# Rope parts of three heads stacked on 96 partitions, swapped weight columns in place of rotations, and taps in another order

## What is computed

```python
proj = h @ w_in
conv_in, c_q, c_kv, k_r, d_q, d_k, d_v = jnp.split(proj, cuts, axis=-1)
y_conv = conv_module(conv_in, ...)     # GLU, 31 causal taps, layer norm, SiLU, product
q = (rms_norm(c_q, q_norm) @ w_uq).reshape(B, S, 6, 64 + 32)
q = concat([q[..., :64], apply_rope(q[..., 64:], pos)])
kv = (rms_norm(c_kv, kv_norm) @ w_ukv).reshape(B, S, 6, 64 + 64)
k = concat([kv[..., :64], apply_rope(k_r, pos) for every head])
y_mla = softmax(q @ k.T / sqrt(96), causal) @ kv[..., 64:]
y_diff = (softmax(q1 @ k1.T - alibi) - lam * softmax(q2 @ k2.T - alibi)) @ d_v
x = x + concat([y_conv, y_mla, y_diff]) @ w_out
# apply_rope: (x1, x2) -> (x1 cos - x2 sin, x1 sin + x2 cos) on the halves of 32
```

## Time and profile before

| | us |
|---|---|
| median of 3 runs | 1302.74 (1300.78 to 1306.17) |
| the profiled execution | 1304.77 |
| its span | 1302.9 |
| PE busy in the span | 1243.3 |
| DVE / ACT / POOL busy | 1020.0 / 822.2 / 144.8 |

### The profile page before, as it was taken

The page is one execution under the profiler, slowest core; times in us unless marked ns, Lnnn a source line. Parts: engine busy times, 40 slices in busy tenths (PEclk is TensorE's granted clock), DMA queues, the critical chain, the costliest instruction groups (busy, mean ns, idle before and its releaser), DMA issues.

```text
span 1302.9 us, 18352 instructions
## 1 busy us (share of the span) xinstructions
PE 1243.3 (95%) x6658; PEld 1052.8 (81%) x6658; DVE 1020.0 (78%) x1107; ACT 822.2 (63%) x862; POOL 144.8 (11%) x139
## 2 busy tenths in 40 slices
PE   6898899999899887999999999999999999999997
PEld 6875799999897676888888888888888888888885
DVE  5886555544568756889989889889889889889886
ACT  5357444444543754777777777677677777777774
POOL 2860000000049102000000000000000000000000
PEclk9888999999899797999999999999999999999999
DMA  9400665555351119999999999999999999999961
GB/s 331 155 15 1 200 201 187 186 176 189 117 178 65 49 46 376 367 369 371 364 366 358 365 359 362 360 369 359 352 374 358 350 377 349 358 372 359 357 238 48
DMA packets 176165, 349.64 MB, mean 268 GB/s; under 512 B 5719, under 2 KB 63637, under 8 KB 176116
## 3 DMA queue, kind: packets, MB, share of 16 engines
q1 hardware_dynamic: 173852, 341.27, 73.9%
q0 software_dynamic: 2064, 7.17, 1.5%
q10 hardware_dynamic: 200, 0.54, 0.1%
HBM read 346.87 MB, written 2.10 MB: 268 GB/s over the span
## 4 chain that ended last, share of the span: by engine, by line
PE 87%; DVE 7%; ACT 3%; issue 2%; DMA 0%; SPq 0%; POOL 0%; POOLq 0%; DVEq 0%; ACTq 0%
PE bank L1482 26%; PE bank L1484 26%; PE bank L1483 26%; PE bank L1797 1%; DVE cv L1127 1%; PE bank L1579 1%; DVE lo_ring L1006 1%; DVE xn L1127 1%; PE bank L1619 1%; ACT hi_ring L690 1%; PE bank L1789 1%; PE bank L1763 1%; PE bank L1778 1%; PE bank L1561 1%; PE bank L1790 1%
## 5 line engine op out<-in xcount | busy, mean ns | idle before, releaser
L1011 DVE TENSOR_TENSOR lo_ring<-raw_m,hi_ring 128x2048 fp32r<-128x2048 f32 x168 | 382.9, 2287 | 53.0 <-ACT hi_ring L696 52.9
L696 ACT ACTIVATE hi_ring<-raw_m 128x2048 fp32r<-128x2048 f32 x168 | 323.0, 1923 | 84.0 <-PE bank L1484 84.0
L1482 PE MATMUL bank<-hi_ring,hT_hi 128*128 128x512 f32 (+2 forms) x896 | 337.2, 376 | 0.0
L1484 PE MATMUL bank<-hi_ring,hT_lo 128*128 128x512 f32 (+2 forms) x896 | 329.5, 368 | 0.0
L1483 PE MATMUL bank<-lo_ring,hT_hi 128*128 128x512 f32 (+2 forms) x896 | 329.1, 367 | 0.0
L1011 DVE TENSOR_TENSOR lo_ring<-raw_a,hi_ring 128x2048 fp32r<-128x2048 f32 x96 | 219.1, 2290 | 32.7 <-ACT hi_ring L696 32.7
L696 ACT ACTIVATE hi_ring<-raw_a 128x2048 fp32r<-128x2048 f32 x96 | 183.4, 1918 | 54.6 <-PE bank L1484 54.6
L1006 DVE TENSOR_TENSOR lo_ring<-raw_a,hi_ring 128x2048 fp32r<-128x2048 f32 (+2 forms) x59 | 132.2, 2244 | 94.8 <-ACT hi_ring L690 94.8
L1482 PEld LDWEIGHTS bank<-hi_ring,hT_hi 128*128 128x128 f32 x896 | 169.6, 189 | 30.3 <-DVE lo_ring L1011 2.4
L1484 PEld LDWEIGHTS bank<-hi_ring,hT_lo 128*128 128x128 f32 x896 | 169.5, 189 | 28.9
L1483 PEld LDWEIGHTS bank<-lo_ring,hT_hi 128*128 128x128 f32 x896 | 169.8, 189 | 27.2 <-issue 0.5
(11 more groups left out here) (277 smaller groups left out, 1409.0 us busy)
## 6 DMA issues: line engine op xcount, KB each, us to landing
raw_m<-in_w_down_exp SPq DMA_DIRECT2D x80, 1024.0 KB, 5.9
raw_a<-in_w_up_exp SPq DMA_DIRECT2D x48, 1024.0 KB, 6.3
raw_m<-in_w_gate_exp SPq DMA_DIRECT2D x48, 1024.0 KB, 6.2
raw_a<-in_w_gate_exp SPq DMA_DIRECT2D x40, 1024.0 KB, 6.2
raw_m<-in_w_up_exp SPq DMA_DIRECT2D x40, 1024.0 KB, 7.2
raw_a<-in_w_in SPq DMA_DIRECT2D x12, 1024.0 KB, 8.0
raw_a<-in_w_gate_dense SPq DMA_DIRECT2D x11, 1024.0 KB, 5.4
raw_a<-in_w_up_dense SPq DMA_DIRECT2D x11, 1024.0 KB, 5.8
```

The lines of the kernel that those rows point to most:

```text
L696: A(hi_of(NA + j), t, ACT.Copy).then_inc(hi_ready, 1)
L1011: V.tensor_tensor(lo_of(NA + j), expert_slot(i, j)[0], hi_of(NA + j).bitcast(F32), ALU.subtract).then_inc(lo_ready, 1)
L1482: M(o, lh, rh, start=start, stop=False)
L1484: return M(o, ll, rh, start=False, stop=stop)
```

## The change

- Queries and keys are kept in parts: `q_nope`, `k_nope` (64 rows a head, two heads on 128 partitions) and `q_rope` (32 rows a head, three heads on 96 partitions). `kr` holds the rope key three times.
- `w_uq` and `w_ukv` come in as `wq_nope`, `wq_rope`, `wk_nope`, `w_v`. POOL copies `wq_rope` with its halves exchanged to `wq_swap`, and a product with it takes the place of the rotation of `q_m`. The sign stands in the sine table.
- `load_small` has 7 DMAs in place of 3, and for layer 0 it stands behind piece 3.
- Each MLA score has four products in place of two.
- The six `bias` tables of layer 0 are made on ACT behind piece 3, no longer on DVE; `setup_lambda` moves from step 4 to step 6 of DVE.
- `TAPS_AT` goes from 0, 0, 8, 9, 8, 7, 5, 2, 1 to 0, 0, 8, 3, 8, 9, 6, 4, 2.

```diff
 N_PARAMS = 6
-MID = 16
+N_SMALL = 7
+MID = 13
+MID_MEAN, MID_VAR, MID_PW = 11, 12, 13
...
-MID_BANK = [0, 1, 2, 3, 0, 1, 2, 3, 0, 1, 2, 3, 0, 7, 7, 7]
-MID_ACT = {0: 1, 1: 2, 2: 3, 3: 4, 5: 5, 6: 6, 10: 8, 11: 9, 12: 10}
-ACT_MID_STEPS = 10
-ROPE_AT = {6: (0, 1), 7: (2,)}
-KEYS_AT = {7: (0, 1, 2)}
-DVE_MID_STEPS = 15
-MID_DVE = {4: 5, 7: 8, 8: 11, 9: 14}
+ACT_MID_STEPS = 7
+DVE_MID_STEPS = 9
...
 OUT_BANK = (5, 6, 4, 3)
-TAPS_AT = [0, 0, 8, 9, 8, 7, 5, 2, 1]
+TAPS_AT = [0, 0, 8, 3, 8, 9, 6, 4, 2]
...
 two[:, K_MASK:K_MASK + 3 * P] = np.where(dist < 0, MASKED, 0.0)
-two[:, K_DIST:K_DIST + 3 * P] = np.maximum(dist, 0)
+two[:, K_DIST:K_DIST + 3 * P] = np.where(dist < 0, -MASKED, dist)
...
 ang = np.arange(T, dtype=np.float32)[None, :] * freq[:, None].astype(np.float32)
-two[:NOPE, K_COS:K_COS + T] = 1.0
-for r in range(2):
-    lo = NOPE + r * half
-    two[lo:lo + half, K_COS:K_COS + T] = np.cos(ang)
-    two[lo:lo + half, K_SIN:K_SIN + T] = np.sin(ang)
+for r in range(3):
+    lo = r * ROPE
+    for a in range(ROPE):
+        two[NOPE + a, K_REP + lo + a] = 1.0
+        two[NOPE + (a + half) % ROPE, K_SWAP + lo + a] = 1.0
+    two[lo:lo + ROPE, K_COS:K_COS + T] = np.tile(np.cos(ang), (2, 1))
+    two[lo:lo + half, K_SIN:K_SIN + T] = -np.sin(ang)
+    two[lo + half:lo + ROPE, K_SIN:K_SIN + T] = np.sin(ang)
...
 sp.dma_start(w_pw[:], a["w_pw"][l].rearrange("(k p) n -> p k n", p=P)).then_inc(small_in, 16)
-sp.dma_start(w_uq[:], a["w_uq"][l].rearrange("(k p) n -> p k n", p=P)).then_inc(small_in, 16)
-sp.dma_start(w_ukv[:], a["w_ukv"][l]).then_inc(small_in, 16)
+for c in range(2):
+    heads = a["w_uq"][l, c * P:(c + 1) * P, :].rearrange("p (h d) -> p h d", h=HEADS)
+    sp.dma_start(wq_nope[:, c], heads[:, :, 0:NOPE]).then_inc(small_in, 16)
+    sp.dma_start(wq_rope[:, c], heads[:, :, NOPE:QD]).then_inc(small_in, 16)
+heads = a["w_ukv"][l].rearrange("p (h d) -> p h d", h=HEADS)
+sp.dma_start(wk_nope[:], heads[:, :, 0:NOPE]).then_inc(small_in, 16)
+sp.dma_start(w_v[:], heads[:, :, NOPE:]).then_inc(small_in, 16)
...
      lambda t, p=p: in_piece_view(t, p))
-if l == 0 and p == 2:
+if l == 0 and p == 3:
     load_small(0)
...
+pool.wait_ge(small_in, 16 * N_SMALL * (l + 1))
+half = ROPE // 2
+for m in range(2):
+    nc.gpsimd.tensor_copy(wq_swap[:, :, :, m * half:(m + 1) * half],
+                          wq_rope[:, :, :, (1 - m) * half:(2 - m) * half]).then_inc(w_swapped, 1)
...
     split(n0 + 3 + p)
+if l == 0 and p == 3:
+    for h in range(HEADS):
+        slope = 2.0 ** (-8.0 * (h + 1) / HEADS)
+        A(bias[:, h, :], dist, ACT.Copy, scale=-slope * HD ** 0.5).then_inc(bias_set, 1)
 if l == 0 and p == 1:
...
 if p == 5:
-    for r3 in range(3):
-        mid(1 + r3)
-        mid_inc(A(q_m[:, 2 * r3:2 * r3 + 2, :],
-                  bank[1 + r3][0:QD, :].rearrange("p (h t) -> p h t", h=2), ACT.Copy))
+    mid(2)
+    mid_inc(A(q_nope[:, 0:2, :], bank[1][:].rearrange("p (h t) -> p h t", h=2), ACT.Copy))
+    mid(3)
+    mid_inc(A(q_nope[:, 2, :], bank[2][:, 0:T], ACT.Copy))
...
 for t in range(TT):
-    mid(5 + t)
+    mid(6 + t)
...
-    act.wait_ge(mid_dve, DVE_MID_STEPS * l + 6)
-    mid_inc(A(k_m[NOPE:QD, :, :], kr[NOPE:QD, :].unsqueeze(1).broadcast_to([ROPE, HEADS, T]),
-              ACT.Copy))
-if p in KEYS_AT:
-    for r3 in KEYS_AT[p]:
-        mid(10 + r3)
-        mid_inc(A(k_m[0:NOPE, 2 * r3:2 * r3 + 2, :],
-                  bank[MID_BANK[10 + r3]][0:NOPE, :].rearrange("p (h t) -> p h t", h=2), ACT.Copy))
+if p == 7:
+    mid(8)
+    mid_inc(A(k_nope[:, 0:2, :], bank[1][:].rearrange("p (h t) -> p h t", h=2), ACT.Copy))
+    mid(9)
+    mid_inc(A(k_nope[:, 2, :], bank[2][:, 0:T], ACT.Copy))
...
 V.tensor_reduce(lam_dot[:], lam_prod[:], AX.X, ALU.add).then_inc(setup_v, 1)
-for h in range(HEADS):
-    slope = 2.0 ** (-8.0 * (h + 1) / HEADS)
-    V.scalar_tensor_tensor(bias[:, h, :], dist, -slope * HD ** 0.5, mask, ALU.mult, ALU.add).then_inc(setup_v, 1)
...
-def rope_q(pairs):
-    for r3 in pairs:
-        pair = q_m[:, 2 * r3:2 * r3 + 2, :]
-        wide = [QD, 2, T]
-        dve.wait_ge(mid_mm, MID * l + 8 + r3)
-        dve.wait_ge(mid_dve, ms_[0])
-        mids(V.tensor_tensor(pair, pair, cos.unsqueeze(1).broadcast_to(wide), ALU.mult))
-        mids(V.tensor_tensor(rot[:], bank[MID_BANK[7 + r3]][0:QD, :].rearrange("p (h t) -> p h t", h=2),
-                             sin.unsqueeze(1).broadcast_to(wide), ALU.mult))
-        dve.wait_ge(mid_dve, ms_[0])
-        mids(V.tensor_tensor(pair, pair, rot[:], ALU.add))
+def rope_k():
+    dve.wait_ge(mid_mm, MID * l + 2)
+    mids(V.tensor_tensor(kr[:], bank[3][0:QD, 0:T], cos, ALU.mult))
+    mids(V.tensor_tensor(rot[:, 0, :], bank[3][0:QD, T:2 * T], sin, ALU.mult))
+    dve.wait_ge(mid_dve, ms_[0])
+    mids(V.tensor_tensor(kr[:], kr[:], rot[:, 0, :], ALU.add))
+def rope_q():
+    wide = [QD, 2, T]
+    dve.wait_ge(mid_mm, MID * l + 6)
+    mids(V.tensor_tensor(q_rope[:], bank[0][0:QD, :].rearrange("p (h t) -> p h t", h=2),
+                         cos.unsqueeze(1).broadcast_to(wide), ALU.mult))
+    mids(V.tensor_tensor(rot[:], bank[3][0:QD, :].rearrange("p (h t) -> p h t", h=2),
+                         sin.unsqueeze(1).broadcast_to(wide), ALU.mult))
+    dve.wait_ge(mid_dve, ms_[0])
+    mids(V.tensor_tensor(q_rope[:], q_rope[:], rot[:], ALU.add))
...
     setup()
-if l == 0 and p == 4:
+if l == 0 and p == 6:
     setup_lambda()
...
-    dve.wait_ge(mid_mm, MID * l + 5)
-    mids(V.tensor_tensor(kr[:], kr[:], cos, ALU.mult))
-    mids(V.tensor_tensor(rot[:, 0, :], bank[0][0:QD, 0:T], sin, ALU.mult))
-    dve.wait_ge(mid_dve, ms_[0])
-    mids(V.tensor_tensor(kr[:], kr[:], rot[:, 0, :], ALU.add))
+    rope_k()
+if p == 6:
+    rope_q()
 if p == 7:
     maxima(0)
-if p in ROPE_AT:
-    rope_q(ROPE_AT[p])
 if p == 8:
...
 else:
-    q, kk = q_m[:, h, :], k_m[:, h, :]
+    r0, g0 = (h % 2) * NOPE, (h % 3) * ROPE
+    q, kk = q_nope[r0:r0 + NOPE, h // 2, :], k_nope[r0:r0 + NOPE, h // 2, :]
+    qr, kkr = q_rope[g0:g0 + ROPE, h // 3, :], kr[g0:g0 + ROPE, :]
 b = bank[S_BANK[u % 3]]
-M(b[:, 0:P], q[:, 0:P], kk[:, 0:P], start=True, stop=True)
-M(b[:, P:3 * P], q[:, P:2 * P], kk[:, :], start=True, stop=True).then_inc(s_mm, 1)
+M(b[:, 0:P], q[:, 0:P], kk[:, 0:P], start=True, stop=k < HEADS)
+if k >= HEADS:
+    M(b[:, 0:P], qr[:, 0:P], kkr[:, 0:P], start=False, stop=True)
+r = M(b[:, P:3 * P], q[:, P:2 * P], kk[:, :], start=True, stop=k < HEADS)
+if k >= HEADS:
+    r = M(b[:, P:3 * P], qr[:, P:2 * P], kkr[:, :], start=False, stop=True)
+r.then_inc(s_mm, 1)
...
     M(bank[0][:, T:2 * T], ones[:], sq_kv[:], start=True, stop=True).then_inc(mid_mm, 1)
+    if l == 0:
+        pe.wait_ge(params_in, 16 * N_PARAMS)
+    M(bank[3][0:QD, 0:T], replicate, kr[:], start=True, stop=True)
+    M(bank[3][0:QD, T:2 * T], swap, kr[:], start=True, stop=True).then_inc(mid_mm, 1)
 if p == 5:
-    pe.wait_ge(small_in, 48 * (l + 1))
-    pe.wait_ge(mid_dve, DVE_MID_STEPS * l + 3)
-    for r3 in range(3):
-        for hh in range(2):
-            h = 2 * r3 + hh
-            for c in range(2):
-                r = M(bank[1 + r3][0:QD, hh * T:(hh + 1) * T], w_uq[:, c, h * QD:(h + 1) * QD],
-                      cq[:, c, :], start=c == 0, stop=c == 1)
-        r.then_inc(mid_mm, 1)
-    mid_start(4)
-    M(bank[0][0:QD, 0:T], rotate, kr[:], start=True, stop=True).then_inc(mid_mm, 1)
+    pe.wait_ge(small_in, 16 * N_SMALL * (l + 1))
+    after_dve(2)
+    for pair in range(HEADS // 2):
+        for c in range(2):
+            r = M(bank[1 + pair // 2][:, (pair % 2) * T:(pair % 2 + 1) * T],
+                  wq_nope[:, c, 2 * pair:2 * pair + 2, :].rearrange("p h d -> p (h d)"), cq[:, c, :],
+                  start=c == 0, stop=c == 1)
+        if pair > 0:
+            r.then_inc(mid_mm, 1)
 if p == 6:
+    after_act(1)
+    for g in range(2):
+        for c in range(2):
+            r = M(bank[0][0:QD, g * T:(g + 1) * T], wq_rope[:, c, 3 * g:3 * g + 3, :].rearrange("p h d -> p (h d)"),
+                  cq[:, c, :], start=c == 0, stop=c == 1)
+    r.then_inc(mid_mm, 1)
+    after_dve(6)
+    pe.wait_ge(w_swapped, 2 * (l + 1))
+    for g in range(2):
+        for c in range(2):
+            r = M(bank[3][0:QD, g * T:(g + 1) * T], wq_swap[:, c, 3 * g:3 * g + 3, :].rearrange("p h d -> p (h d)"),
+                  cq[:, c, :], start=c == 0, stop=c == 1)
+    r.then_inc(mid_mm, 1)
     for t in range(TT):
-        mid_start(5 + t)
-        wv = w_ukv[:].rearrange("p (h n) -> p h n", h=HEADS)[:, :, NOPE:]
-        M(bank[1 + t][:, 0:HEADS * MV], ckv[:, t * P:(t + 1) * P], wv, start=True, stop=True
-          ).then_inc(mid_mm, 1)
-if p in ROPE_AT:
-    for r3 in ROPE_AT[p]:
-        mid_start(7 + r3)
-        M(bank[MID_BANK[7 + r3]][0:QD, :], rotate,
-          q_m[:, 2 * r3:2 * r3 + 2, :].rearrange("p h t -> p (h t)"), start=True, stop=True
-          ).then_inc(mid_mm, 1)
-if p in KEYS_AT:
-    for r3 in KEYS_AT[p]:
-        mid_start(10 + r3)
-        for hh in range(2):
```

(15 more changed lines are left out.)

48 lines of the change are left out of this document (26 added, 22 removed).

## The result

| | before | changed |
|---|---|---|
| median, us | 1303.4 (4 runs, 1300.78 to 1306.17) | 1295.86 (4 runs, 1295.3 to 1296.88) |
| ratio | | 0.9945, 95% interval 0.9925 to 0.9966 |
| the profiled execution, its span | 1304.77, 1302.9 | 1295.9, 1294.1 |

The forecast was 1296.2, and the total is met. The terms that make it up are not: two of them lie outside the bounds that they were given, and a gain that was not in the sum at all helps to make up the total. The profile shows where.

The account below looks back on a forecast made before the run. PE idles in the mixers behind DVE, and POOL is late next. Layer 0 -4.25, dense start +0.8 and layer 1 -3.1 give -6.55, so 1296.2 us on the median's scale; 8 in 10 between 1290 and 1303.5.

Parts of the forecast that it names:

- The join: DVE's join in the mixers' first stage starts when POOL ends: 3.95 us earlier in layer 0, 2.8 in layer 1.
- POOL's own gain: POOL's taps run faster with fewer rope operations beside them: about 0.3 us for each, some 0.6 in all.
- Behind the join: From DVE's join to the MLA slots, waits for PE vanish: 0.8 us gained a layer, between 0 and 1.1.
- the backlog: PE's queued scores and values behind the join, about 0.5 us, gone because PE idles while DVE waits for POOL.
- The MLA products: Second mixer stage: doubled score products in six MLA units cost 0.5 us net a layer, between 0.1 and 1.0.
- the pair of slot 3: Two units on different groups of 32 rows, 1.59 us where 2.6 was due, read as products on different rows overlapping.
- the rival of the low clock in the slots: MLA slots stay at low clock, plus 9.5 us in each layer, 1315 us in total; chance 0.10.
- Small loads: Weight loads in runs of 128 and 256 bytes cost 2.5 us more, upper end 5.2; hidden in layer 0.
- the cover of 3.1: Layer 0: slack between piece 4 landing at about 26.4 and ACT's split at 29.49, hiding 2.5 us of load cost.
- dense start: Layer 1's small loads ahead of the dense pieces make the dense part start 0.8 us later, between 0 and 3.5.
- Free of charge: Six biases on ACT fit its pause before piece 4, and POOL's two copies its idle 22.82 us; no cost.
- POOL slowed by 4 us in each layer: Rival: POOL gains nothing and two further jumps of 2 us come in its taps; about 1303.5 us, chance 0.10.

Follow-up runs that it names:

- e8: The kernel before, run once more unchanged for a second profiled execution; 1303.45 us.
- e5: The kernel before with only the new order of DVE's taps and the lambda setup two pieces later; 1298.21 us, ratio 0.9958.
- e3: The changed kernel with layer 1's seven small loads issued behind the eighth dense piece, no longer ahead of the first; 1295.74 us.
- e7: The changed kernel with MLA score products on all 128 and 96 rows, made right by key tiles with zeros in other heads' rows; 1293.58 us, ratio 0.9926.
- e6: The changed kernel with unread products on constants where PE would idle, ahead of scores(1) and of the norm transposes behind both mixers; 1297.66 us.
- e9: The changed kernel with the old order of DVE's taps over the nine pieces; 1296.97 us over 12 widely scattered runs, ratio 0.9952.
- e11: The changed kernel with zero-padded key tiles and layer 1's small loads behind the eighth dense piece; 1290.72 us, ratio 0.9903.
- e1: The changed kernel without the second product (32 rope rows) of each MLA score, so scores lack their rope part; 1293.52 us.
- e12: The changed kernel with zero-padded key tiles, late layer 1 small loads, and 20 of the second block's taps on POOL, not 22; 1288.3 us, ratio 0.9887.

## Why the prediction came out

**The join** (predicted -3.95 and -2.8). The reading of POOL as late next was right: in both layers the join waits for it, 3.16 and 3.56 us. In layer 0 it came 5.1 us earlier, 4.0 against e8. The size of POOL's own gain was off: 0.6 forecast, 53.75 to 51.65 us measured in layer 0 (2.1) and 0.9 in layer 1. In e5, which has the new order and the old rope work, POOL's run is 54.0 and 54.4. So what the change takes away is worth 1.9 to 2.4 us of POOL's run, not 0.3 for each of two triples. Not all of it is shown to be the rope operations. By an estimate from the timelines, tap by tap, the taps beside them are 1.1 to 1.4 us slower in all before and in e5, and 0 to 0.4 in the changed kernel; the rest lies beside the splits and has no cause here.

**Behind the join** (-0.8 a layer, bounds 0 to 1.1). This step left its bounds: the changed kernel gained 3.2 us in layer 0 and 0.8 in layer 1; e3 and e7 gained 2.5 and more in both. What was missing is the clock. From the join to the first MLA score, layer 0 before, layer 0 now and layer 1 now:

```profile
91.70:107.53 15.83, 15.83 (x58) 10.86 (x58) 10.55 (x51) 11.51 (x47) 0.00 (x0) 0.50 0.00 0
```

```profile
86.59:99.20 12.61, 11.96 (x49) 8.18 (x48) 10.30 (x49) 8.88 (x35) 0.00 (x0) 0.61 0.00 0
422.24:437.27 15.03, 14.00 (x48) 9.62 (x48) 10.39 (x49) 10.31 (x41) 0.56 (x1) 0.50 0.10 35
```

PE is busy nearly all the time, so it is the bound, and length times granted clock is 7.9, 7.7 and 7.5 us (7.5 to 8.2 in every kernel without the fillers of e6). At the same clock of 0.50 the gain is 0.8 us (layer 1; 0.8 and 0.9 in e9 and e11), which is what the backlog was priced at. The rest is the granted clock, which the sum held at its value before. The clock falls earlier against the join, at 82.8 where the join is at 86.59 (91.0 and 91.70 before), and part of the low stretch passes while DVE and PE wait for POOL. How long it stays low is not repeatable: 13.7 us in layer 0 and 20.5 in layer 1 in the changed kernel, 17.1 and 13.7 in e3, which is the same kernel up to there but for when the small loads are issued. Even the kernel before was 1.6 us faster there in one layer in e8. So that the new order brings the clock back sooner is likely and not shown.

**The MLA products** (+0.5 a layer, 0.1 to 1.0). The other step that failed: +2.5 and +2.8, and e1 shows it. The error is in one sentence. I read the pair of slot 3, 1.59 us for 2.6, as products on different rows that overlap, and carried that over to products on 64 and 32 rows. It doesn't hold where the number of rows changes from product to product. It also has the heads wrong: the rows meet for three of the six, not for two. And I let PE's idle in the slots cover the rest; with 1.42 us a unit the six add 8.5, and PE's waits in the slots before sum to 6.6. In the other direction the rival of the low clock in the slots was wrong: they run at 1.00.

```profile
108.00:112.00 4.00, 4.00 (x18) 2.50 (x19) 2.73 (x11) 1.86 (x7) 0.00 (x0) 1.00 0.00 0
```

**Small loads.** The short runs cost 2.2 us (2.5 forecast). In layer 0 the cover of 3.1 should have left 0.6; instead ACT's fifth split waits a little:

```profile
29.79 1.91 ACT L695 ACTIVATE hi_ring<-raw_a 128x2048 fp32r<-128x2048 f32 x1 [0.45 <-DMA raw_a<-in_w_in]
```

That is 0.3 later than before; four more issues on SP were not in the sum. At the dense start the wait cost 0.9 us (6.84 for 5.94; 0.8 forecast). The stretch up to layer 1 is longer by 1.0 more; I put that to the half clock, which was not in the sum, since e5 has the same 3.4 us of it, no such wait, and 1.1 more than before. The nearness of 2.5 and 2.2 is in part luck. The window that 8.7 ns a run came from shows only 93 packets under 512 bytes by the DMA view (14 to 17 us, before), where the changed kernel has 3026 (21 to 24 us): the short runs of `wr` and the lambdas show no packets of their size there, only 189 larger ones on the software queue.

**Free of charge.** The biases on ACT took 2.58 us ahead of an idle of 0.56, so they cost nothing, as said. So did the copies on POOL.

**Signs.** Of the signs that were named, these came: no idle before the query products, full clock to 79 us, a join released by POOL behind a wait of over 3 us, MLA slots at full clock. These did not: the join of layer 0 is at 86.59 and not between 87 and 89, ACT's fifth split has a DMA wait, and its wait for the second dense piece stayed at 1.09 us; the one for the first grew, from 0.63 to 2.65. And POOL's run of 51.65 in layer 0 lies below the 52 to 55 that was set as the mark of being wrong (layer 1: 52.5): the size of POOL's gain is what failed there, not its place as the bound.

**Slips in the working.** The query products before were at half clock only to 60.3 us, for 5.0 of their 7.88. And for POOL slowed by 4 us in each layer the terms give 1296.2 + 8 = 1304.2, not 1303.5. Neither moves the forecast.

**Not in the sum at all.** 2.1 us in the experts' stage (e8), and 1.2 where the clock came back sooner behind the router in this execution.

Added up with the profiled span, forecast and measured: layer 0 -4.25 and -5.8, dense start +0.8 and +1.9, layer 1 -3.1 and -1.55, experts 0 and -3.3; together -6.55 and -8.8 (-7.5 against e8). The total was met because too small a gain behind the join, too small a cost in the slots and an unseen gain in the experts' stage cancel out: that the number came so close is luck.

What the change is worth, part by part: the order of the taps 5.2 us alone. The stacked rope parts and the swapped weights bring the end of layer 0's projection from 87.82 to 81.03 (e9) and POOL's run is 2 us shorter with them; they give 5.3 us back in the MLA slots of the two layers. With the order in place they add 2.3, about what the 2.1 in the experts' stage give.

## What to carry to other kernels

When an operation is split in two to save copies, count the price on the engine that will be full afterwards, and look in the timeline whether a weight load starts ahead of its product or with it: here each product on 64 and 32 rows in turn cost 0.2 us more than on 128 and 96, and rows of zeros were cheaper than a change of rows. Where an engine is busy throughout a stretch, multiply its length by the granted clock before giving a difference a cause; here that turned a gain of 3.2 us into one of 0.8 and a matter of the clock. Before adding gains of two parts, ask which engine is late next in each; if it is the same one, the gains don't add. A change that nobody waits for (the late loads) may be worth something once another one has made its place the tight one (2.9 us here by the medians), so such pieces are worth trying again together.

## What the runs showed of the hardware

- In products on 64 and 32 rows in turn no weight load was hidden: 0.42, 0.41, 0.63 and 0.62 us between starts, where 128 and 96 rows gave 0.22, 0.22, 0.43 and 0.43. In e1 a load from 64 rows to 64 rows was hidden (0.11 us ahead), the ones from 128 to 64 and back were not.
- From the join to the first MLA score PE was busy nearly throughout, and length times granted clock was the same at either length: 7.9 us where it took 15.8 at 0.50 (before) and 8.0 where it took 14.3 at 0.56 (e8).
- The same product (L1789 before, L1805 now) took 392 to 404 ns in the three executions with the old data layout and 389 in the eleven with the new one.
- POOL's run of 43 instructions took 1.9 to 2.4 us longer in e5 than in the changed kernel, beside two more triples of rope operations on DVE.
- The same kernel showed 64.9 and 61.5 us of half clock in two executions; at the dense start the clock was low for 6.8 us in e3 and 3.4 in e5, and full in the kernel before (both executions), e11 and e12, with idles of 1.45 and 1.03 us ahead in all of them.
- 16 DMA engines, fully busy, moved 196 GB/s in runs of 128 and 256 bytes and 359 in runs of 768 to 1536.
